# A second home for six eighths of the gate matrix of odd experts, the layer loop written out, and the router on column groups

## The chip, the cores and the metric

The kernel runs on one core of one Trainium2 chip. The metric is the time of one execution on the device in microseconds, the median of several runs. The engines named below are TensorE (PE in the profile, with its weight loads as PEld), VectorE (DVE), ScalarE (ACT), GpSimd (POOL) and SyncE (SP), which here only issues DMAs. SBUF is the on-chip memory of 128 partitions, PSUM the accumulators of TensorE, with eight banks of 512 float32 per partition. All data is float32.

## The reference

Two layers of a bidirectional encoder over 256 tokens of width 1024. Each layer adds a mixing block (latent attention with 16 heads, and a gated long convolution of order 2) and then a mixture of 16 experts, in which each expert picks its own 32 tokens:

```python
def expert_choice_ffn(h, router_w, wg, wu, wd):
    B, S, D = h.shape
    C = max(1, EC_CAPACITY_FACTOR * S // N_EXPERTS)
    aff = jax.nn.softmax((h @ router_w).astype(jnp.float32), axis=-1)
    gate, idx = lax.top_k(jnp.swapaxes(aff, 1, 2), C)
    flat_idx = idx.reshape(B, N_EXPERTS * C)
    xs = jnp.take_along_axis(h, flat_idx[..., None], axis=1).reshape(B, N_EXPERTS, C, D)
    a = jnp.einsum('becd,edf->becf', xs, wg)
    u = jnp.einsum('becd,edf->becf', xs, wu)
    o = jnp.einsum('becf,efd->becd', jax.nn.silu(a) * u, wd) * gate[..., None].astype(h.dtype)
    o = o.reshape(B, N_EXPERTS * C, D)
    return jax.vmap(lambda oi, ii: jnp.zeros((S, D), h.dtype).at[ii].add(oi))(o, flat_idx)

# per layer: x = x + merged @ w_out[l]
#            x = x + expert_choice_ffn(rms_norm(x, norm2_w[l]), router_w[l], wg[l], wu[l], wd[l])
```

Each expert has three matrices of 1024 x 1408, 1024 x 1408 and 1408 x 1024, that is 5632 KB each. With 2 x 16 experts the weights of the experts are most of what the kernel reads.

## The kernel before

**Memory.** `ring` (2 x 11264 columns per partition) holds units of the mixing block's weights first, and during the experts the gate matrix `wg` in its first half and the up matrix `wu` in its second. `region` (`R`, 12288 columns) holds q, k, v and the convolution's spectra first, and the down matrix `wd` during the experts (11264 columns). `attnT` (`aT`) holds the attention's output and later the normed x, transposed, which is the router's operand. `work` (`W`) is scratch of the mixing block; its last readers and writers before the experts are ScalarE's squares for the second norm (L885).

**Order.** Each engine has its own program, written out by hand with semaphores, and runs it in order. All five programs have a loop over the layers (`Fori(0, DEPTH)`) on registers. Inside, PE and VectorE loop over four groups of four experts, ScalarE over 16 experts, and SyncE over experts 1 to 15. Thresholds of waits that depend on the layer are computed in registers.

**Around the experts.** PE computes `merged @ w_out` (L644), transposes x (L629), and multiplies it with the router's weights: eight matmuls of 16 x 256 that accumulate in one bank (L654). VectorE copies the result (L1206), PE transposes it back (L660), VectorE takes the maximum (L1208, L1211), ScalarE the exponentials (L908), and VectorE picks the 32 best tokens of each expert (L1223 to L1234). Per group PE gathers the tokens of four experts with a matmul (L681). Per expert PE computes the gate product and the up product (both L695), each as eight steps of four matmuls on four column groups (a fp32 matmul counts as two instructions in the trace, so a product has 64), then two transposes of the selection (L703), three of the hidden rows (L709), the down product (L719) and the product that adds the rows to x (L734, L1273).

**SyncE's queue.** All weights are asked for by SyncE, in this order: gate(0) in two halves (L269) when w_out's first unit is used, up(0) (L272) when its second is used, then for e = 1 to 15 the first half of gate(e) after half of gate product e-1 (`gate_half`), its second half after the whole product (`gate_done`), up(e) after up product e-1 (`up_done`), and down(e) (L278) after down product e-1 (`o_psum`) in three pieces. down(0) is asked for earlier, before the last unit of w_out. At the end of a layer SyncE asks for the next layer's small tables, and for w_lat (L257) once `gate_done` has counted expert 15.

**Layer boundary.** After the last addition to x ScalarE squares x (L769), takes the root (L772), VectorE inverts it (L980) and scales x (L983), and PE transposes (L358).

## Time and profile before

| | us |
|---|---|
| median of 3 runs | 2113.52 |
| lowest and highest | 2112.22, 2116.02 |
| the profiled execution | 2112.32 |
| its span, first to last instruction | 2110.5 |
| PE busy in it | 1606.2 (76%) |
| DVE busy | 508.7 (24%) |
| ACT busy | 287.6 (14%) |
| moved by DMA | 644.83 MB, 306 GB/s over the span |

The page's map of the span in 40 slices shows two equal halves, one per layer. In each, PE is busy nine tenths and more while the DMA moves little, and then for some 600 us the DMA moves about 430 GB/s while PE is busy five or six tenths. The granted clock of PE is near full in the first kind of stage and eight or nine tenths in the second. Busy time of an engine says how long it had an instruction in it, not whether anyone waited for it; the chain that ended last says that. A wait named "issue" is time in which an engine waited for nothing that the profile shows.

### The profile page before, as it was taken

The page shows a single profiled execution, that of the slowest core. Times are in us where ns is not written, and L with a number is a line of the kernel's source. Part 1 is how long each engine was busy: PE and PEld are TensorE (multiplying, and loading weights), DVE is VectorE, ACT ScalarE, POOL GpSimd, SP SyncE. Part 2 cuts the span into 40 slices and gives each one's busy share as a digit, 9 for nine tenths or more (in the row PEclk, how much of TensorE's full clock was granted, in tenths as well). Part 3 has the DMA queues.
Part 4 walks back from the last instruction along what each step waited for, and adds up shares of the span by engine and source line. Part 5 has one row for each costly group of instructions (what it writes and reads, how often), then busy time and mean ns, then how long its engine had stood idle before and what let it go on. Part 6 is the DMA issues. An engine that isn't in the chain of part 4 may idle for free.

```text
span 2110.5 us, 23405 instructions
## 1 busy us (share of the span) xinstructions
PE 1606.2 (76%) x9552; PEld 909.9 (43%) x9552; DVE 508.7 (24%) x1057; ACT 287.6 (14%) x594; POOL 45.7 (2%) x24
## 2 busy tenths in 40 slices
PE   7999999876466566666689999997865665665665
PEld 4687688432232132232256866884322222321322
DVE  2654541111111111111126545402111111111111
ACT  2233200200000000000022332002000000000000
POOL 0300000000000000000002000000000000000000
PEclk9999999988788888878899999999887887888888
DMA  7522024679999999999945220246899999999997
GB/s 282 195 85 100 1 80 190 245 319 430 435 423 430 430 427 430 432 429 426 426 149 199 80 100 1 80 189 258 341 434 426 426 430 434 423 430 430 427 430 319
DMA packets 36352, 644.83 MB, mean 306 GB/s; under 512 B 3984, under 2 KB 4880, under 8 KB 6160
## 3 DMA queue, kind: packets, MB, share of 16 engines
q1 hardware_dynamic: 35472, 638.84, 72.2%
q10 hardware_dynamic: 768, 4.29, 0.7%
q8 instruction: 96, 1.57, 0.3%
q14 instruction: 16, 0.13, 0.0%
HBM read 642.07 MB, written 1.05 MB: 305 GB/s over the span
## 4 chain that ended last, share of the span: by engine, by line
PE 49%; DMA 42%; issue 4%; DVE 3%; DVEq 1%; SPq 1%; ACT 1%; ACTq 0%
DMA region<-w_down_dram 27%; DMA ring<-w_up_dram 15%; PE ps L695 7%; PE ps L394 7%; PE ps L619 5%; PE ps L461 5%; PE ps L719 3%; PE ps L644 3%; PE ps L552 2%; PE ps L681 2%; PE ps L587 2%; PE ps L577 2%; PE ps L422 2%; PE ps L484 1%; PE ps L439 1%
## 5 line engine op out<-in xcount | busy, mean ns | idle before, releaser
L695 PE MATMUL ps<-ring,uT 128*32 128x384 f32 (+1 forms) x4096 | 437.7, 567 | 296.8 <-DMA ring<-w_gate_dram 147.6
L695 PEld LDWEIGHTS ps<-ring,uT 128*32 128x32 f32 x4096 | 182.9, 130 | 550.6 <-issue 205.6
L719 PE MATMUL ps<-region,uT 128*32 128x512 f32 x1408 | 175.8, 596 | 34.9 <-DVE uT L1266 22.2
L1262 DVE TENSOR_TENSOR uT<-uT,ps 128x256 f32<-128x256 f32 x32 | 13.5, 421 | 699.4 <-PE ps L695 699.4
L394 PE MATMUL ps<-xnT,ring 128*128 128x256 f32 x768 | 178.3, 380 | 4.5 <-DVE uT L942 2.9
L394 PEld LDWEIGHTS ps<-xnT,ring 128*128 128x128 f32 x768 | 140.6, 190 | 24.1 <-DVE uT L942 4.5
L734 PE MATMUL ps<-uT 128*128 128x512 f32 x256 | 124.3, 618 | 28.8 <-ACT uT L926 28.8
L920 ACT ACT_TABLE_LOAD x32 | 41.1, 1283 | 631.3 <-PE ps L695 631.3
L461 PE MATMUL ps<-xnT,ring 128*128 128x256 f32 x512 | 115.0, 380 | 0.0
L719 PEld LDWEIGHTS ps<-region,uT 128*32 128x32 f32 x1408 | 44.5, 109 | 143.9 <-issue 105.3
L1273 DVE TENSOR_TENSOR x<-x,ps 128x512 f32<-128x512 f32 x128 | 87.9, 687 | 64.4 <-PE ps L734 64.4
L681 PE MATMUL ps<-uT,xnT 128*128 128x128 f32 x256 | 50.5, 381 | 68.2 <-issue 65.6
L461 PEld LDWEIGHTS ps<-xnT,ring 128*128 128x128 f32 x512 | 96.5, 190 | 13.7 <-issue 0.8
L734 PEld LDWEIGHTS ps<-uT 128*128 128x128 f32 x256 | 40.7, 188 | 114.9 <-issue 73.0
L681 PEld LDWEIGHTS ps<-uT,xnT 128*128 128x128 f32 x256 | 48.7, 294 | 73.7 <-issue 73.7
L1268 DVE COPY uT<-ps 128x512 f32<-128x512 f32 x32 | 22.1, 691 | 194.5 <-PE ps L719 194.5
L619 PE MATMUL ps<-uT,ring 128*128 128x256 f32 x256 | 57.9, 379 | 0.0
L619 PE MATMUL ps<-attnT,ring 128*128 128x256 f32 x256 | 57.9, 379 | 0.0
L644 PE MATMUL ps<-ring,uT 128*128 128x512 f32 x128 | 55.6, 592 | 0.0
L924 ACT ACTIVATE uT<-ps 128x256 f32<-128x256 f32 x32 | 12.3, 384 | 311.6 <-PE ps L703 311.6
L619 PEld LDWEIGHTS ps<-uT,ring 128*128 128x128 f32 x256 | 48.6, 190 | 6.6
L619 PEld LDWEIGHTS ps<-attnT,ring 128*128 128x128 f32 x256 | 48.6, 190 | 6.6
(195 smaller groups left out, 1368.1 us busy)
## 6 DMA issues: line engine op xcount, KB each, us to landing
ring<-w_gate_dram SPq DMA_DIRECT2D x64, 2816.0 KB, 28.4
ring<-w_up_dram SPq DMA_DIRECT2D x32, 5632.0 KB, 32.8
region<-w_down_dram SPq DMA_DIRECT2D x64, 2048.0 KB, 30.6
ring<-units_dram SPq DMA_DIRECT2D x34, 2048.0 KB, 8.0
region<-w_down_dram SPq DMA_DIRECT2D x32, 1536.0 KB, 37.2
ring<-w_lat_dram SPq DMA_DIRECT2D x4, 1344.0 KB, 20.6
ring<-w_q_b_dram SPq DMA_DIRECT2D x2, 2304.0 KB, 29.1
region<-filt_dram ACTq DMA_DIRECT2D x4, 512.0 KB, 11.9
```

Of the source, the lines that this page charges most:

```text
L394: m = mm(bank(b % 2, S), unit8(n)[:, i, j * P:(j + 1) * P], xnT[:, i], start=i == 0, stop=i == DB - 1)
L422: m = mm(bank((3 + g) % 7), latT[:, i, t * P:(t + 1) * P], m2[:, i, c * 512:(c + 1) * 512], start=i == 0, stop=i == QB - 1)
L461: m = mm(dst, unit8(7 + 4 * (i // 4) + g)[:, k, i % 4 * P:(i % 4 + 1) * P], xnT[:, k], start=k == 0, stop=k == DB - 1)
L552: m = mm(bank(5 + f), cst[:, C_F + t * NF + f * P:C_F + t * NF + (f + 1) * P], hflt[:, t], start=t == 0, stop=t == SB - 1)
L577: m = mm(bank(2 + f), cst[:, C_F + t * NF + f * P:C_F + t * NF + (f + 1) * P], z_t[:, c, t], start=t == 0, stop=t == SB - 1)
L619: m = mm(dst, unit8(n)[:, k, j * P:(j + 1) * P], (aT if g == 2 else uT)[:, k], start=k == 0, stop=k == DB - 1)
L644: m = mm(bank(4 + 2 * c + t), mT[:, k, t * P:(t + 1) * P], unit8(n)[:, k], start=k == 0, stop=k == DB - 1)
L681: m = mm(bank(i // 4, P, (i % 4) * P), xn2[:, t, i * P:(i + 1) * P], pick[:, t], start=t == 0, stop=t == SB - 1)
L695: m = mm(bank(b, QW[j], rows=CAP, row0=CAP * j), xs[:, i, q * CAP:(q + 1) * CAP], w[:, i, j * FT:j * FT + QW[j]], start=i == 0, stop=i == ...
L719: m = mm(bank(c, rows=CAP, row0=CAP * j), hT[:, b * P + CAP * j:b * P + CAP * (j + 1)], wd[:, CT * b + j, c * 512:(c + 1) * 512], start=b ...
L734: mm(bank(6 + k % 2), gselT[:, t * P:(t + 1) * P], o_sb[:, c * 512:(c + 1) * 512], start=True, stop=True).then_inc(s["y2_psum"], 1)
L1273: tt(xc, xc, bank(6 + k % 2), ALU.add).then_inc(s["x_dve"], 1)
```

## The change

The gate matrix of an expert is cut at six eighths: "a" are the weight rows i = 0 to 5 (8448 columns per partition), "b" the last two (2816 columns). Even experts keep a in the ring. Odd experts have it in a second home that starts behind the down matrix in `region` and runs through a spare area, `attnT` and `work`, which are laid out as one tensor with `region` for that. b and the up matrix keep their one place. SyncE asks for a(0), b(0) and up(0) as before, for a(1) once the router's matmul and the second norm are done (`lgT_psum`, `norm2_rms`), and then per expert for b, up, down and the a of the next expert. PE waits for a and b apart; `gate_a` takes the place of `gate_half`. To make room, the scratch for dynamic DMA descriptors is given as 2048 bytes.

The router's eight matmuls go to four column groups (weights padded from 16 to 32 columns), two on each; VectorE copies 128 rows, and a matmul with a constant matrix (C_SUM) adds the four groups and transposes in one. The loop over layers is a Python loop on every engine, and SyncE's loop over experts too.

```diff
@@ build
-        R = sb("region", 12 * 1024)
+        region = sb("region", 12 * 1024 + SPARE + DB * S + 3072)
+        R = region[:, 0:12 * 1024]
+        aT_t = region[:, 12 * 1024 + SPARE:12 * 1024 + SPARE + DB * S]
+        W = region[:, 12 * 1024 + SPARE + DB * S:12 * 1024 + SPARE + DB * S + 3072]
...
-        wg = ring[:, 0:SLOT].rearrange("p (i f) -> p i f", i=DB)
-        wu = ring[:, SLOT:2 * SLOT].rearrange("p (i f) -> p i f", i=DB)
+        wg_a = (ring[:, 0:A_COLS], region[:, NF_TILES * D:NF_TILES * D + A_COLS])
+        wg_b = ring[:, A_COLS:SLOT]
...
@@ block.sync
-            with sp.Fori(0, DEPTH) as L:
+            for L in range(DEPTH):
...
-                def load_gate(e, half):
-                    cols = slice(SLOT // 2 * half, SLOT // 2 * (half + 1))
-                    sp.dma_start(ring[:, cols], w_gate[L * E + e, :, cols]).then_inc(s["wg_in"], 16)
+                def load_gate_a(e):
+                    sp.dma_start(wg_a[e % 2], w_gate[L * E + e, :, 0:A_COLS]).then_inc(wga_in[e % 2], 16)
+
+                def load_gate_b(e):
+                    sp.dma_start(wg_b, w_gate[L * E + e, :, A_COLS:SLOT]).then_inc(s["wgb_in"], 16)
...
-                load_gate(0, 0)
-                load_gate(0, 1)
+                load_gate_a(0)
+                load_gate_b(0)
                 unit_is_used(16)
                 load_up(0)
-                with sp.Fori(1, E) as e:
-                    sp.wait_ge(s["gate_half"], L * E + e)
-                    load_gate(e, 0)
+                sp.wait_ge(s["lgT_psum"], L + 1)
+                sp.wait_ge(s["norm2_rms"], L + 1)
+                load_gate_a(1)
+                for e in range(1, E):
                     sp.wait_ge(s["gate_done"], L * E + e + FREE)
-                    load_gate(e, 1)
+                    load_gate_b(e)
                     sp.wait_ge(s["up_done"], L * E + e + FREE)
                     load_up(e)
                     sp.wait_ge(s["o_psum"], L * E + e + FREE)
                     load_down(e)
+                    if e < E - 1:
+                        sp.wait_ge(s["gate_a"], L * E + e)
+                        load_gate_a(e + 1)
@@ block.tensor
-                    m = mm(bank(4, S, rows=E), fvec[:, W_RT + i * E:W_RT + (i + 1) * E], aT[:, i],
-                           start=i == 0, stop=i == DB - 1)
+                    m = mm(bank(4, S, rows=EP, row0=EP * (i % 4)), fvec[:, W_RT + i * EP:W_RT + (i + 1) * EP], aT[:, i],
+                           start=i < 4, stop=i >= 4)
...
-                    m = tp(bank(5, E, t * E), lgT[:, t * P:(t + 1) * P], ident[0:E, 0:E])
+                    m = mm(bank(5, E, t * E), lgT[:, t * P:(t + 1) * P], cst[:, C_SUM:C_SUM + E], start=True, stop=True)
...
+                        pe.wait_ge(wga_in[q % 2], 8 * L * E + 32 * g + 16 * (q // 2) + 16)
+                        pe.wait_ge(s["sil_act"], n + FREE)
+                        for i in range(IA):
+                            m = product(2, wg[q % 2], i)
+                        m.then_inc(s["gate_a"], 1)
+                        pe.wait_ge(s["wgb_in"], 16 * (n + 1))
+                        for i in range(IA, DB):
+                            m = product(2, wg[q % 2], i)
+                        m.then_inc(s["gate_done"], 1)
@@ block.vector
-                copy(lgT, bank(4, S, rows=E)).then_inc(s["lgT_dve"], 1)
+                copy(lgT, bank(4, S)).then_inc(s["lgT_dve"], 1)
@@ kernel
-    nc = bacc.Bacc("TRN2", target_bir_lowering=False, num_devices=1)
+    nc = bacc.Bacc("TRN2", target_bir_lowering=False, num_devices=1, dynamic_dma_scratch_size=2048)
```

SyncE's program from gate(0) on, before. "ring<-w_gate_dram 128x5632" is half a gate matrix, and an ISA row is a wait of its own; the rows from the branch on are the loop over experts.

```order
L269 DMA ring<-w_gate_dram 128x5632 [waits wout_psum]
L269 ISA
L269 DMA ring<-w_gate_dram 128x5632
L247 REGISTER_ALU
L272 DMA ring<-w_up_dram 128x11264 [waits wout_psum]
L296 UNCONDITIONAL_BRANCH
L296 ISA
L269 ISA [waits gate_half]
L269 DMA ring<-w_gate_dram 128x5632
L299 REGISTER_ALU
L269 ISA [waits gate_done]
L269 DMA ring<-w_gate_dram 128x5632
```

The same place after. "128x8448" is a, "128x2816" is b, and "region<-w_gate_dram" is the second home.

```order
L278 DMA ring<-w_gate_dram 128x8448 [waits wout_psum]
L281 DMA ring<-w_gate_dram 128x2816
L284 DMA ring<-w_up_dram 128x11264 [waits wout_psum]
L278 DMA region<-w_gate_dram 128x8448 [waits norm2_rms,lgT_psum]
L281 DMA ring<-w_gate_dram 128x2816 [waits gate_done]
L284 DMA ring<-w_up_dram 128x11264 [waits up_done]
L290 DMA region<-w_down_dram 128x4096 [waits o_psum]
L290 DMA region<-w_down_dram 128x4096
L290 DMA region<-w_down_dram 128x3072
L278 DMA ring<-w_gate_dram 128x8448 [waits gate_a]
L281 DMA ring<-w_gate_dram 128x2816 [waits gate_done]
```

a(1) stands behind up(0) with waits for the router and the norm and no wait for a product, and a(2) behind down(1).

VectorE at the layer boundary, before: the last additions to x, the ends of the group loop and of the layer loop. The next instruction of the following layer is L980, 449 rows further up.

```order
L1273 TENSOR_TENSOR x<-x,ps 128x512
L1238 REGISTER_ALU
L1238 COMPARE_AND_BRANCH
L977 REGISTER_ALU
L977 COMPARE_AND_BRANCH
```

And after:

```order
L1298 TENSOR_TENSOR x<-x,ps 128x512
L1263 REGISTER_ALU
L1263 COMPARE_AND_BRANCH
L1005 RECIPROCAL small<-small 128x2
L1008 TENSOR_SCALAR region<-x,small 128x1024 x2
```

The reciprocal that starts a layer (L980 before, L1005 after) now follows the group loop directly.

## Rows read from the trace of the kernel before

**Rows 1.** The page: chain that ended last, shares by engine and line.

```profile
PE 49%; DMA 42%; issue 4%; DVE 3%; DVEq 1%; SPq 1%; ACT 1%; ACTq 0%
DMA region<-w_down_dram 27%; DMA ring<-w_up_dram 15%; PE ps L695 7%; PE ps L394 7%; PE ps L619 5%; PE ps L461 5%; PE ps L719 3%; PE ps L644 3%; PE ps L552 2%; PE ps L681 2%; PE ps L587 2%; PE ps L577 2%; PE ps L422 2%; PE ps L484 1%; PE ps L439 1%
```

**Rows 2.** Windows: us, busy us of engines, PEclk, DMA share, GB/s.

```profile
440.00:640.00 200.00, 131.68 (x1027) 53.52 (x1025) 28.44 (x57) 14.62 (x28) 0.00 (x0) 0.84 1.00 429
...
1500.00:1700.00 200.00, 131.38 (x981) 52.36 (x974) 29.95 (x58) 14.64 (x26) 0.00 (x0) 0.84 1.00 429
```

**Rows 3.** Pieces of that chain: start us, us, what.

```profile
466.18 8.02 PE ps L695 x34
...
1010.52 37.23 DMA region<-w_down_dram
```

**Rows 4.** Timeline of SyncE's DMA issues: start us, us, line, transfer, count.

```profile
409.20 0.33 SPq L272 DMA_DIRECT2D ring<-w_up_dram  x1
435.84 2.91 SPq L269 DMA_DIRECT2D ring<-w_gate_dram  x2
443.44 0.33 SPq L272 DMA_DIRECT2D ring<-w_up_dram  x1
...
1028.22 0.85 SPq L257 DMA_DIRECT2D ring<-w_lat_dram  x2
...
1486.98 2.91 SPq L269 DMA_DIRECT2D ring<-w_gate_dram  x2
1494.59 0.33 SPq L272 DMA_DIRECT2D ring<-w_up_dram  x1
```

**Rows 5.** Windows between router and expert 0; columns of rows 2.

```profile
422.00:424.00 2.00, 0.00 (x0) 0.00 (x0) 1.77 (x5) 0.00 (x0) 0.00 (x0) 0.50 0.83 360
424.00:436.00 12.00, 9.53 (x76) 8.02 (x79) 2.63 (x8) 0.00 (x0) 0.00 (x0) 0.73 0.01 1
436.00:438.00 2.00, 2.00 (x28) 1.00 (x24) 0.00 (x0) 0.00 (x0) 0.00 (x0) 1.00 0.64 169
...
1476.00:1488.00 12.00, 10.17 (x86) 8.34 (x90) 2.38 (x6) 0.00 (x0) 0.00 (x0) 0.76 0.05 13
```

**Rows 6.** Timeline, layer 0's router: start, us, what, [idle before <-releaser].

```profile
410.78 3.61 PE L654 MATMUL ps<-attnT,fvec 128*16 128x256 f32 x16 [0.17 <-issue]
411.33 0.84 ACT L892 ACTIVATE attnT<-ps,fvec 128x256 f32<-128x256 f32 x2
412.55 1.28 ACT L908 ACT_TABLE_LOAD   x1
412.57 0.17 DVE L1204 RECIPROCAL small<-small 128x2 f32<-128x2 f32 x1 [1.11 <-ACT small L903]
...
414.99 0.27 PE L660 MATMUL ps<-consts,uT 16*128 16x16 f32 x2 [0.60 <-DVE uT L1206]
...
415.56 0.16 DVE L1211 TENSOR_TENSOR small<-small 128x2 f32<-128x2 f32 x1
...
432.86 10.52 PE L695 MATMUL ps<-ring,uT 128*32 128x384 f32 x128 [0.97 <-DVE uT L1248]
```

**Rows 7.** Timeline, program's start and layer boundary; columns of rows 6.

```profile
11.42 0.17 DVE L980 RECIPROCAL small<-small 128x2 f32<-128x2 f32 x1 [10.54 <-ACT small L772]
...
1057.59 0.30 ACT L772 ACTIVATE small<-small,consts 128x2 f32<-128x2 f32 x1
1060.73 0.17 DVE L980 RECIPROCAL small<-small 128x2 f32<-128x2 f32 x1 [5.52 <-issue]
...
1062.46 3.38 PE L358 MATMUL ps<-consts,region 128*128 128x128 f32 x16 [7.97 <-DVE region L983]
```

**Rows 8.** Waits up to 432 us: who <- releaser: us, times, longest.

```profile
PE ps L495 <- issue: 0.6, 1, 0.6
DVE uT L1241 <- issue: 0.3, 1, 0.3
```

**Rows 9.** The page: the weights' DMA queue: packets, MB, share.

```profile
q1 hardware_dynamic: 35472, 638.84, 72.2%
```

More of the change, by code:

```diff
@@ L107, in build @@
         uT_t = sb("uT", 24 * S)
-        aT_t = sb("attnT", DB * S)
-        W = sb("work", 3072)
         cst = sb("consts", C_N)
@@ L311, in _ @@
         def _(pool):
-            with pool.Fori(0, DEPTH) as L:
+            for L in range(DEPTH):
                 pool.wait_ge(s["qkw_scaled"], L + 1)
@@ L350, in _ @@
                 pe.sem_inc(s[n], FREE)
-            with pe.Fori(0, DEPTH) as L:
+            for L in range(DEPTH):
                 pe.wait_ge(s["consts_in"], 16)
@@ L687, in _, with product @@
                         n = L * E + g * GROUP + q
-                        for w, b, arrived, read, done in ((wg, 2, "wg_in", "sil_act", "gate_done"),
-                                                          (wu, 3, "wu_in", "hid_dve", "up_done")):
-                            pe.wait_ge(s[arrived], (32 if w is wg else 16) * (n + 1))
-                            pe.wait_ge(s[read], n + FREE)
-                            for i in range(DB):
-                                for j in range(CT):
-                                    m = mm(bank(b, QW[j], rows=CAP, row0=CAP * j), xs[:, i, q * CAP:(q + 1) * CAP],
-                                           w[:, i, j * FT:j * FT + QW[j]], start=i == 0, stop=i == DB - 1)
-                                if w is wg and i == DB // 2 - 1:
-                                    m.then_inc(s["gate_half"], 1)
-                            m.then_inc(s[done], 1)
+                        def product(b, w, i):
+                            for j in range(CT):
+                                m = mm(bank(b, QW[j], rows=CAP, row0=CAP * j), xs[:, i, q * CAP:(q + 1) * CAP],
+                                       w[i][:, j * FT:j * FT + QW[j]], start=i == 0, stop=i == DB - 1)
+                            return m
+                        pe.wait_ge(wga_in[q % 2], 8 * L * E + 32 * g + 16 * (q // 2) + 16)
[7 more added lines that the diff above has]
+                        m.then_inc(s["gate_done"], 1)
+                        pe.wait_ge(s["wu_in"], 16 * (n + 1))
+                        pe.wait_ge(s["hid_dve"], n + FREE)
+                        for i in range(DB):
+                            m = product(3, wu, i)
+                        m.then_inc(s["up_done"], 1)
                         pe.wait_ge(s["gsel_dve"], n + 1)
@@ L756, in _ @@
                 act.sem_inc(s[n], FREE)
-            with act.Fori(0, DEPTH) as L:
+            for L in range(DEPTH):
                 load_sqrt_table()
@@ L976, in _ @@
             dve.sem_inc(s["x_dve"], X_FREE)
-            with dve.Fori(0, DEPTH) as L:
+            for L in range(DEPTH):
                 dve.wait_ge(s["norm1_rms"], L + 1)
```

23 lines of the change are left out of this document (17 added, 6 removed).

## The prediction

> **What bounds the kernel now.** I read the chain that ended last first: 49% of it is PE and 42% is DMA, and the DMA part is the expert weights, w_down and w_up [rows 1]. So there are two kinds of stage. Next the windows by stage: from 440 us to the end of layer 0's experts, and again from 1500 us in layer 1, the 16 DMA engines are busy 1.00 of the time and move 429 GB/s, while PE is busy about two thirds [rows 2]. The reader is to see that nothing PE does there matters as long as the queue never runs dry: the experts are a stream of bytes. One expert is 3 x 5632 KB = 17.3 MB, which at 429 GB/s is 40.3 us; the last piece of w_down in layer 0 lands 37 us after PE began to wait for it, at 1010.52 + 37.23 = 1047.75 [rows 3]. The other stages, some 420 us a layer, are PE's, and the DMA engines have little to do in them.
>
> So I look for the moment from which the stream runs without a gap, and for what comes before it. In the list of SyncE's DMA issues, layer 0 asks for up(0) at 409.20, and then for nothing until 435.84, when PE is half through gate product 0 [rows 4]. The windows show the consequence: the stream ends at about 423.7 (share 0.83 in 422 to 424), is 0.01 from 424 to 436, and is back in 436 to 438; in layer 1 the share of 1476 to 1488 is 0.05 [rows 5]. That is 13 us of idle queue in each layer, directly ahead of a stage that is nothing but queue. Every us of it that is filled with weights comes off the end.
>
> **The second home for the gate.** Call the six eighths "a" (4224 KB, 10.1 us at 429 GB/s) and the last two "b" (1408 KB, 3.4 us). Before, gate(1) (13.45 us) starts with the request at 435.84. After, a(1) may be asked for once the router's matmul has read attnT and the second norm has left "work". These end at about 414.4 and 412.5 [rows 6], well before up(0) has streamed out at 423.7, so a(1) queues behind up(0) without a gap and is through at 423.7 + 10.1 = 433.8. b(1) still waits for gate product 0 to end, and up(1) for up product 0. In the trace up product 0 ends 10.58 us after gate product 0 begins: begun at 432.86 [rows 6], up(1) asked for at 443.44 [rows 4]. b(1), asked for half-way through these 10.58 us, needs 1.4 us until its first data (as between the request at 435.84 and the 169 GB/s of 436 to 438 [rows 5]) and 3.4 us of stream, and so it is through by the time at which up(1) is asked for, or a few tenths before or behind it. From the request for up(1) on, the after-kernel streams without a gap.
>
> So before, the unbroken stream starts with a request at 435.84 and has gate(1) in it; after, it starts with a request at 443.44 less what the router gives (below, 1.45), at 442.0, and gate(1) is out of it. Gain: 13.45 - (442.0 - 435.84) = 7.3 us. Only 5.85 of it is the second home; it can't be the whole 10.1 us of a(1), because up(1) has a single home and becomes the next late thing. Layer 1 has the same distances (requests at 1486.98 and 1494.59 [rows 4], so 7.61 us between them as in layer 0). Two layers: 14.6 us.
>
> From expert 2 on I cost the second home at nothing. A load of up or down waits for the same event as before, b for the same as before's second half, and a(e+1) for an event that is long past when SyncE reaches it; the stream has no gap before [rows 2] and each request comes no later against it. Six DMAs per expert before, six after. What is queued behind SyncE's new waits is only expert weights.
>
> **The router on column groups.** Before, eight matmuls of 256 columns take 3.61 us one after the other, 0.45 each [rows 6]. After, four of them run side by side. The price is that of the expert products, which already do this: 16 steps of four (128 x 384) in 10.52 us, 0.66 a step, which is no more than one product of 384 columns at the router's pace (0.68). So a step of four costs 0.45. The first step starts at 410.78 as before, the second waits for ScalarE's copies, which end at 411.33 + 0.84 = 412.17, and ends at about 412.7 instead of 414.4. VectorE's reciprocal holds the next copy until 412.74 [rows 6]. The copy of 128 x 256 instead of 16 x 256 has as many elements per partition, and I take it to last as long. The two transposes (0.27 us) become two matmuls with 128 x 128 weights and 16 columns: at least nothing more, at most twice as long; I take 0.1. The exponentials need lmax (415.72 before) and the table load, which ends at 412.55 + 1.28 = 413.83 [rows 6]: with lmax at about 414.2 the table is not yet the next late thing. Saved: 1.45 us from here to gate product 0, counted above already. The top-k and the gather behind it are untouched.
>
> **The layer loop written out.** At the layer boundary ScalarE has the root of the norm at 1057.89, but VectorE takes it at 1060.73, with 5.52 us idle before it put down to "issue"; at the start of the program the same reciprocal waits for nothing but ScalarE's root [rows 7]. VectorE branches back over the whole layer there. Written out, the branch is gone and the 2.8 us with it, once. PE's transposes wait for exactly this [rows 7], and w_lat, asked for at 1028.22 [rows 4] and next in the stream behind w_down, has landed by then (2688 KB, 6.4 us of stream behind 1047.75). The inner loops over groups stay.
>
> The loop's register arithmetic goes too, some 40 instructions on PE per layer. Outside the experts the trace shows hardly any idle time put down to "issue" (0.6 us on PE, 0.3 on VectorE, each once up to 432 us [rows 8]), so I count zero, and at most 1 us a layer. From the other side a longer program could stall where it did not: one stall like VectorE's is 2.8 us. Both layers are straight code between the inner loops, and layer 0 is that already without such a stall, so zero again.
>
> The Trainium skill bears on both sides of this in "Runtime: NRT & Kernel Launch", section on the mechanics of instruction fetch: a sequencer streams straight code in blocks of 256 instructions, mostly hidden, and a taken branch to a target outside its two blocks waits for a fetch. By it the 2.8 us come back whole and rival 1 below falls away; the boundary's row agrees as far as VectorE goes, and ScalarE, which branches there too, shows no such wait. I keep the rival, since no trace shows straight code of twice this length.
>
> The larger tables (64 KB of router weights a layer, 8 KB of constants) come long before they are used.
>
> **Sum.** 14.6 + 2.8 = 17.4 us. The profiled execution took 2112.32 us with a span of 2110.5, so 2094.9 and 2093.1. The median of the runs, 2113.52, is 1.2 above the profiled one: 2096.1.
>
> **Rivals.** (1) The branch's time comes back in another form at the boundary (fetching new code, or PE not ready): 14.6 alone, 2098.9. Against it speaks the program's start [rows 7]. (2) More comes off: the waits of rows 8 and a few small ones on ScalarE and VectorE, up to 2 or 3 us a layer: about 2091. For it speaks that all four engines shed register work; against it that these rows are small.
> (3) The clock. PE runs the gather at the low level and is back at the high one only shortly before gate product 0: the granted clock is 0.73 over 424 to 436 and 1.00 in 436 to 438 [rows 5]. If the shorter router burst leaves PE at the low clock for products 0, a product takes 8.02 us as it does in mid-stream [rows 3] and not 5.3, up(1) is asked for 5.5 us later, and of 7.3 a layer 1.8 is left: 2 x 1.8 + 2.8 = 6.4 us, 2107.1. The same time comes out if a(1) is not in fact early, since then only router and branch are left (5.7). Against it speaks that the gather, the work that precedes the rise, is not changed.
> (4) Slower: a gap in the stream at every expert. The program gives the descriptors' scratch less room (2048 bytes, set by hand) and changes the piece sizes. If that made the queue drain once per expert, each drain costs the 1.4 us from request to first data, and from 17.4 / 30 = 0.6 us per expert on the change loses. One drain costs 30 x 1.4 = 42 us, so 2113.5 + 24.6 = 2138. Against it: all weights go by a queue of kind hardware_dynamic [rows 9], and SyncE runs several loads ahead of the landing in the trace.
> "SBUF — State Buffer" of the Trainium skill, section on the size of SBUF, calls this scratch the ring of the software-generated descriptors; by that page the weights' queue does not touch it and rival 4 has no ground but the piece sizes; no run here has shown it, and its chance stands as it is.
>
> **How the numbers follow.** Forecast 0.70 with 2091 to 2101 of its own (1 us of error a layer in each of the two terms, and 2 us between runs); rival 1 0.08; rival 2 0.10; rival 3 0.07; rival 4 0.04; 0.01 for anything else. Rivals 1 and 2 lie inside or at the edge, so 2089 to 2102 leaves out rivals 3 and 4 and the tails, about 2 in 10. A difference of 0.2% (4.2 us) is about what a measurement tells from none. Faster by more: the forecast, rivals 1 to 3, 0.93 after their tails; within it 0.03; slower 0.04.
>
> **What will show it.** Right: requests for a(1) near 413 and up(1) near 442.0, DMA share near 1.00 until 433.8, some 4 us idle and then 1.00; 429 GB/s after that; last w_down of layer 0 at about 1040.4 instead of 1047.75; at the boundary the reciprocal within 0.1 us of the root. Wrong: a share below 1.00 in mid-stream (rival 4), the clock at 0.5 in gate product 0 (rival 3), an "issue" wait at the boundary (rival 1), or stages outside the experts that are shorter by more than 1 us (rival 2).

## The result, and the profile after

| us | before | after |
|---|---|---|
| median | 2113.89 | 2086.93 (4 runs, 2084.02 to 2088.7) |
| the profiled execution | 2112.32 | 2086.2 |
| its span | 2110.5 | 2084.4 |

The ratio is 0.9877, with an interval of 0.9864 to 0.9889: 27.0 us less where 17.4 were forecast. 2086.9 lies below the range. So 9.6 us more came off than the steps of the prediction add up to.

Three stretches of each trace show where. The first runs from a layer's first transposes to the request for up(1), the second from there to the start of the last expert's product that adds rows to x, the third from there to the transposes of the next layer.

| us, layer 0 / layer 1 | before | after |
|---|---|---|
| transposes to the request for up(1) | 430.30 / 432.13 | 427.45 / 427.55 |
| from there to the last expert's addition | 607.16 / 606.89 | 601.01 / 596.59 |
| layer boundary | 11.86 | 8.97 |

The first stretch became shorter by 2.9 and 4.6 us, where the router's term is 1.45 in each layer.

The page of the kernel after, the map of the span, the queues and the chain that ended last:

```profile
span 2084.4 us, 22376 instructions
...
PEclk9999999988878888887899999999988888788888
DMA  7522024599999999999955220246999999999997
...
q1 hardware_dynamic: 35472, 638.98, 73.2%
...
q8 instruction: 57, 0.93, 0.2%
...
PE 49%; DMA 46%; DVE 2%; ACT 1%; issue 1%; DVEq 1%; ACTq 0%; SPq 0%
```

Against [rows 1], "issue" fell from 4% to 1%. The queue q8, which brings code, moved 57 packets, and in the kernel before:

```profile
q8 instruction: 96, 1.57, 0.3%
```

SyncE's DMA issues after (start us, us, queue, line, transfer, count), layer 0 and then layer 1, to set against [rows 4]:

```profile
408.83 0.33 SPq L284 DMA_DIRECT2D ring<-w_up_dram  x1
412.63 0.33 SPq L278 DMA_DIRECT2D region<-w_gate_dram  x1
436.04 0.33 SPq L281 DMA_DIRECT2D ring<-w_gate_dram  x1
441.20 0.33 SPq L284 DMA_DIRECT2D ring<-w_up_dram  x1
...
1478.73 0.33 SPq L284 DMA_DIRECT2D ring<-w_up_dram  x1
```

a(1) is asked for at 412.63, b(1) at 436.04 and up(1) at 441.20; 413, half-way to up(1), and 442.0 were forecast. The windows after (columns of [rows 2]):

```profile
424.00:426.00 2.00, 1.62 (x7) 1.65 (x8) 0.10 (x1) 0.00 (x0) 0.00 (x0) 0.50 0.94 406
426.00:434.00 8.00, 7.03 (x72) 5.48 (x75) 1.89 (x4) 0.00 (x0) 0.00 (x0) 0.91 0.95 408
434.00:436.00 2.00, 2.00 (x31) 1.02 (x25) 0.00 (x0) 0.00 (x0) 0.00 (x0) 1.00 0.00 0
...
440.00:442.00 2.00, 1.57 (x17) 0.54 (x9) 0.61 (x2) 0.38 (x1) 0.00 (x0) 1.00 0.51 211
442.00:444.00 2.00, 1.30 (x11) 0.55 (x15) 0.52 (x1) 0.00 (x0) 0.00 (x0) 1.00 1.17 360
440.00:640.00 200.00, 135.59 (x1028) 50.94 (x1020) 31.17 (x62) 15.02 (x27) 0.00 (x0) 0.86 1.00 427
1500.00:1700.00 200.00, 124.01 (x929) 47.20 (x925) 27.24 (x54) 14.04 (x25) 0.00 (x0) 0.84 1.00 430
```

The hole of 12 us in [rows 5] is filled up to 434. What is left is 434 to 436 and a dip to 0.51 before up(1). The clock is 1.00 in gate product 0, so rival 3 is out, and the stream runs at 427 and 430 GB/s, so rival 4 is out as far as this trace goes. At the boundary (timeline, columns of [rows 6]):

```profile
1049.03 0.30 ACT L797 ACTIVATE small<-small,consts 128x2 f32<-128x2 f32 x1
1049.36 0.17 DVE L1005 RECIPROCAL small<-small 128x2 f32<-128x2 f32 x1 [2.54 <-ACT small L797]
...
1051.18 3.65 PE L374 MATMUL ps<-consts,region 128*128 128x128 f32 x16 [5.09 <-DVE region L1008]
```

The reciprocal waits for the root alone. In [rows 7] it stood 2.8 us behind it.

The request, the filled hole and the boundary are the forecast. The largest part of what is left is in a place that the prediction never went to. PE's gather opens each round of the group loop (L681 before, L697 after). In the kernel before, at the three group boundaries of layer 0:

```profile
572.87 0.55 PE L681 MATMUL ps<-uT,xnT 128*128 128x128 f32 x1 [5.57 <-issue]
578.61 6.23 PE L681 MATMUL ps<-uT,xnT 128*128 128x128 f32 x31 [5.19 <-issue]
...
735.79 0.55 PE L681 MATMUL ps<-uT,xnT 128*128 128x128 f32 x1 [6.11 <-issue]
741.12 5.24 PE L681 MATMUL ps<-uT,xnT 128*128 128x128 f32 x31 [4.77 <-issue]
...
898.07 0.55 PE L681 MATMUL ps<-uT,xnT 128*128 128x128 f32 x1 [5.82 <-issue]
903.55 5.91 PE L681 MATMUL ps<-uT,xnT 128*128 128x128 f32 x31 [4.93 <-issue]
```

PE stands for 11 us at each with nothing to wait for. Packets of the code queue q8 lie in these waits: at the first boundary the trace has them at 569.8 and 576.2, each 1.0 us long, and PE goes on at 572.87 and 578.61. The kernel after at the same places:

```profile
560.62 3.81 PE L697 MATMUL ps<-uT,xnT 128*128 128x128 f32 x32 [1.37 <-DVE uT L1266]
...
726.38 5.57 PE L697 MATMUL ps<-uT,xnT 128*128 128x128 f32 x27 [6.32 <-issue]
...
889.14 6.64 PE L697 MATMUL ps<-uT,xnT 128*128 128x128 f32 x32 [6.57 <-issue]
```

The waits of PE, summed (who <- releaser: us, times, longest), before and then after:

```profile
PE ps L681 <- issue: 65.6, 12, 6.1
```

```profile
PE ps L697 <- issue: 13.1, 3, 6.6
```

Twelve waits at six boundaries have become three at two (6.3, 6.6 and 0.2 us), and layer 1 has none. PE has slack at these places (the experts are a stream of bytes), so 65.6 us of PE can't be 65.6 us of the program. What they cost the stream had to be measured.

### The profile page after: what moved, and what is told of

It reads as the page before. It is cut to its first block, busy times and chain, and to the rows that moved or that the text cites. A ratio compares the mean times of both kernels' runs of the same rounds, so it can differ in the third digit from the quotient of the medians.

```text
span 2084.4 us, 22376 instructions
## 1 busy us (share of the span) xinstructions
PE 1585.8 (76%) x9556; PEld 893.2 (43%) x9556; DVE 508.3 (24%) x1057; ACT 287.4 (14%) x594; POOL 45.7 (2%) x24
## 4 chain that ended last, share of the span: by engine, by line
PE 49%; DMA 46%; DVE 2%; ACT 1%; issue 1%; DVEq 1%; ACTq 0%; SPq 0%
DMA ring<-w_up_dram 43%; PE ps L707 12%; PE ps L410 7%; PE ps L635 5%; PE ps L477 5%; PE ps L660 3%; PE ps L568 2%; PE ps L603 2%; PE ps L593 2%; DMA region<-w_down_dram 2%; PE ps L438 2%; PE ps L500 1%; PE ps L455 1%; PE ps L744 1%; PE ps L383 1%; PE ps L524 1%
## 5 line engine op out<-in xcount | busy, mean ns | idle before, releaser
L707 PE MATMUL ps<-ring,uT 128*32 128x384 f32 (+1 forms) x3328 | 361.7, 559 | 288.3 <-DMA ring<-w_up_dram 254.5
L707 PEld LDWEIGHTS ps<-ring,uT 128*32 128x32 f32 x3328 | 146.8, 129 | 489.3 <-DMA ring<-w_up_dram 274.2
L707 PE MATMUL ps<-region,uT 128*32 128x384 f32 (+1 forms) x768 | 83.9, 571 | 46.2 <-DMA region<-w_gate_dram 46.2
L744 PEld LDWEIGHTS ps<-region,uT 128*32 128x32 f32 x1408 | 44.1, 109 | 151.4 <-issue 103.6
L707 PEld LDWEIGHTS ps<-region,uT 128*32 128x32 f32 x768 | 34.2, 130 | 98.0 <-DMA region<-w_gate_dram 57.8
L635 PE MATMUL ps<-region,ring 128*128 128x256 f32 x256 | 57.9, 379 | 0.0
L697 PE MATMUL ps<-uT,xnT 128*128 128x128 f32 x256 | 38.9, 323 | 21.1 <-issue 13.1
L951 ACT ACTIVATE uT<-ps 128x512 f32<-128x512 f32 x32 | 19.1, 597 | 237.2 <-PE ps L744 237.2
```

The lines of the kernel that those rows point to most:

```text
L635: m = mm(dst, unit8(n)[:, k, j * P:(j + 1) * P], (aT if g == 2 else uT)[:, k], start=k == 0, stop=k == DB - 1)
L707: m = mm(bank(b, QW[j], rows=CAP, row0=CAP * j), xs[:, i, q * CAP:(q + 1) * CAP], w[i][:, j * FT:j * FT + QW[j]], start=i == 0, stop=i == ...
L744: m = mm(bank(c, rows=CAP, row0=CAP * j), hT[:, b * P + CAP * j:b * P + CAP * (j + 1)], wd[:, CT * b + j, c * 512:(c + 1) * 512], start=b ...
```

## The experiments

Theory after the traces: PE's group loop doesn't fit in PE's store of code in the kernel before. After every branch back code is fetched again, and that costs the weights' stream a little each time. The change moved the loop in the program and so made it fit, in the profiled execution in layer 1 and at one boundary of layer 0. Rivals: the second home gives more than I worked out; the router gives more; fewer instructions of the layer loop help everywhere. Each group of experiments has its own measurement of the kernel before beside it, and its median moved between 2111.58 and 2113.89; differences between kernels of two groups are uncertain by that much.

How the loop lies can be counted in the compiled programs. One round is 1600 instructions with one gate home and 1598 with two; before, it stands at 3526 to 5125 of PE's program, after at 3468 to 5065 and 8525 to 10122. The Trainium skill, in "Runtime: NRT & Kernel Launch", section "Instruction fetch mechanics", gives PE room for 2048 instructions, filled in blocks of 256. So many instructions touch seven or eight such blocks, by where they start. Where the blocks begin I could only fit: with an offset of 52 instructions, which puts a block's edge behind the first matmul of the gather, where PE's second wait stands in the rows of before, the loop of before touches eight and those of after seven, the one of layer 0 by a hair (6.99 blocks from its first block's edge, and 6.75 in layer 1). 2048 instructions are eight blocks, and yet a loop over eight did not stay in any run below; why is open.

**The layer loop written out, alone.** The kernel before with `for L in range(DEPTH)` on all engines:

```diff
-            with pe.Fori(0, DEPTH) as L:
+            for L in range(DEPTH):
```

> The kernel before with nothing changed but the loops: the layer loop written out on all five engines and SyncE's loop over experts too. One gate home, old router. Theory A (what the forecast missed lies in the loops): about 4 us at the layer boundary (it was 3.96 in the trace of after, not 2.8), 1 us a layer outside the experts, and PE's stalls at the group boundaries (11 to 12 us of issue in each before, in two of six after) gone with some 1.3 us of stream each: together 9 to 12 us, so 2102 to 2105. Theory B (the missed part lies in the second home): only 2.8 to 4 us, so 2110 to 2111, and the stalls at the group boundaries stay.

Measured: 2100.74 against 2112.36, ratio 0.9945 (0.9931 to 0.9958), that is 11.6 us less and not 2.8. The boundary is 8.97 as after, the stretch of the experts 602.17 / 602.44, so 4.7 us a layer less, the code queue 39 packets, and no gather waits for issue.

**The second home, alone.** All of the change's `block.sync` and its products, with loops and router as before.

> The second home alone: layer loop on registers as before on all engines, old router; the scratch is 2048 bytes here too, since the room is needed. Theory A: 2 x 5.85 = 11.7 us, so 2102, with PE's stalls at the group boundaries as before and 429 GB/s. Theory B (the early request of a keeps the stream fuller all through): 17 to 21 us, so 2093 to 2097.

Measured: 2102.76 against 2112.36, ratio 0.9963 (0.9949 to 0.9978). Stretch of the experts 601.60 / 601.69, so 5.4 us a layer less, where 5.85 was worked out; boundary 11.77, 96 packets. The medians differ by 9.6 us, where 2 x 5.4 is 10.8. The stalls are there as before.

**The second home with its early request taken away.** The kernel after, in which a(1) is asked for only when gate product 0 has ended:

```diff
-                sp.wait_ge(s["lgT_psum"], L + 1)
-                sp.wait_ge(s["norm2_rms"], L + 1)
+                sp.wait_ge(s["gate_done"], L * E + 1 + FREE)
                 load_gate_a(1)
```

> The kernel after, but a(1) is asked for only when gate product 0 is done, directly ahead of b(1); everything else stays, the second home too. If the gain is the filled idle time, the stream starts with a(1) and b(1) at about 436.0 and reaches up(1) at 436.0 + 1.4 + 13.45 = 450.9 instead of 442.6: 8.3 us a layer are lost, so 2086.9 + 16.6 = 2103.5. If the second home gains in mid-stream, less is lost, 2090 to 2098.

Measured: 2104.68 against 2112.36, ratio 0.996 (0.9944 to 0.9976), 7.7 us below the kernel before where the kernel after is 27.0 below in the first measurement and 23.0 in the repeat further down: 15 to 19 us more. The stretch of the experts rises to 604.69 / 604.66 from the 596.6 that it has without stalls: 8.1 us a layer. Here a(1), 10.1 us of stream, is wholly behind the gap, so the early request is what the second home gives, and the layout by itself nothing: an expert takes 40.2 us from landing to landing here as in the kernel with one home and no stall.

**The code of the kernel before, moved by 20 instructions.** Here lies the test of the theory. The layer loop stays on registers, and PE gets 20 idle instructions at its start:

```diff
             with pe.Fori(0, DEPTH) as L:
+                for _ in range(20):
+                    pe.sem_inc(s["pad_pe"], 1)
```

> The kernel before with 20 idle instructions (increments of an unused semaphore) on PE at the start of a layer, where PE waits for x anyway. All loops stay. They shift PE's loop over the four groups (1600 instructions) by 20 places against the blocks of 256 in which its code is fetched. Theory F: the loop covers eight blocks before and seven when shifted, and only then stays in PE's buffer; so the stalls of 11 us at the six group boundaries vanish, the instruction queue moves about 42 packets instead of 96, and the stream gains 1.57 us at each boundary: 9.4 us, 2103.0. Theory G (the register arithmetic or the outer loop itself costs it): nothing changes, 2112.4.

Measured: 2102.73 against 2113.16, ratio 0.9954 (0.9938 to 0.9969). Work was added and 10.4 us came off. Stretch of the experts 602.51 / 602.50, 42 packets, boundary 12.36. From 562 to 1054 us, the last three rounds of layer 0, its code queue moves no packet at all; in the kernel before it moves nine in each of these rounds. The gathers at the group boundaries of this kernel:

```profile
570.62 3.81 PE L682 MATMUL ps<-uT,xnT 128*128 128x128 f32 x32 [1.43 <-DVE uT L1242]
...
731.69 3.81 PE L682 MATMUL ps<-uT,xnT 128*128 128x128 f32 x32 [1.43 <-DVE uT L1242]
```

**The other way: the written-out loop moved onto eight blocks.** The first experiment's kernel with 40 and 65 idle instructions:

```diff
+                for _ in range((40, 65)[L]):
+                    pe.sem_inc(s["pad_pe"], 1)
```

> The kernel with only the loops written out (2100.7 us), with 40 idle instructions on PE at the start of layer 0 and 65 at that of layer 1, so that PE's group loop covers eight blocks again in both layers. Theory F: stalls at all six boundaries come back, about 93 packets, 9.4 us slower, 2110. Theory G: 2100.7, no stall.

Measured: 2112.52 against 2113.16, ratio 0.9999 (0.9989 to 1.0008): all that the first experiment gained is gone. The experts take 606.76 / 606.71, the code queue 94 packets, and the stalls are back, after the ninth matmul this time, since the edge lies elsewhere in the loop:

```profile
572.78 2.26 PE L682 MATMUL ps<-uT,xnT 128*128 128x128 f32 x9 [6.58 <-issue]
577.93 5.28 PE L682 MATMUL ps<-uT,xnT 128*128 128x128 f32 x23 [2.89 <-issue]
```

The 65 idle instructions also cost at the boundary, which is 13.10 here and was 8.97. So about 4.1 us of this kernel is the padding's, and the stalls' share is the 4.6 + 4.3 us of the two stretches of experts. Together that is 13.0, and the medians differ by 11.8.

**Is it PE's lateness, or the fetch?** At a stall PE is 11 us late, so requests that hang on its products could be late too. Three memsets ahead of the last expert's additions in each group make PE late in the kernel whose loop fits:

```diff
+                        if q == GROUP - 1:
+                            for _ in range(3):
+                                nc.vector.memset(W[:, :], 0.0)
+                                dve.drain()
```

> The kernel with only the loops written out, with three memsets of the dead scratch (3072 columns each, 2 to 3 us) on VectorE ahead of the additions of the last expert of each group: PE is held up at every group boundary for 6 to 10 us, but fetches nothing. It tells what in a stall costs the stream. If it is the late requests of PE (a gap in the queue), the time between the landings around a boundary grows from 80.4 by 1.6 us for two experts, as in the kernel before. If it is the fetched code on the same DMA rings, the landings stay at 40.2 us each and only the delay of the last group of each layer shows in the time: 2100.7 plus twice the delay, 2113 to 2121.

Measured: 2118.95 against 2113.16, ratio 1.0034 (1.0019 to 1.0048); the stretch of experts 612.93 / 612.91, 10.6 us longer than in the first experiment. All of that is the last group's delay, which nothing hides: from the request for up(1) to the last landing of w_down it takes 599.4 us in both layers, as against 599.3 in the first experiment and 604.3 / 604.0 in the kernel before. Between the groups PE is as late as in a stall (from its last additions to its next gate product it takes 20.4 to 22.7 us, in the kernel before 21.5 to 22.7, in the first experiment 10.3 to 10.6), and the stream doesn't notice. The first row shows PE's wait at the third group boundary of layer 0, and the others the additions to x of experts 11, 12 and 13, which follow the landing of their last w_down:

```profile
900.15 3.78 PE L734 MATMUL ps<-uT 128*128 128x512 f32 x4 [8.72 <-DVE x L1277]
```

```profile
889.45 1.98 PE L734 MATMUL ps<-uT 128*128 128x512 f32 x4 [0.89 <-ACT uT L926]
...
930.81 3.88 PE L734 MATMUL ps<-uT 128*128 128x512 f32 x8 [0.89 <-ACT uT L926]
...
969.80 3.88 PE L734 MATMUL ps<-uT 128*128 128x512 f32 x8 [0.90 <-ACT uT L926]
```

The same three in the kernel before, and then in the kernel with the layer loop written out:

```profile
888.37 3.88 PE L734 MATMUL ps<-uT 128*128 128x512 f32 x8 [0.89 <-ACT uT L926]
...
929.54 3.88 PE L734 MATMUL ps<-uT 128*128 128x512 f32 x8 [0.90 <-ACT uT L926]
...
970.35 3.88 PE L734 MATMUL ps<-uT 128*128 128x512 f32 x8 [0.94 <-ACT uT L926]
```

```profile
886.29 3.88 PE L734 MATMUL ps<-uT 128*128 128x512 f32 x8 [0.89 <-ACT uT L926]
...
926.41 3.88 PE L734 MATMUL ps<-uT 128*128 128x512 f32 x8 [0.90 <-ACT uT L926]
...
966.62 3.88 PE L734 MATMUL ps<-uT 128*128 128x512 f32 x8 [0.90 <-ACT uT L926]
```

Two experts take 969.80 - 889.45 = 80.35 us with PE held up and 80.33 with PE free, but 81.98 with the stall. So a late PE costs the stream nothing, and what comes with the stall costs 1.6 us a boundary; by the stretches of the experts it is 4.3 to 5.0 a layer. In the kernel before, 96 - 42 = 54 packets more are fetched than with the 20 idle instructions, nine for each of six boundaries. They are not all fetched at the boundary: in the second round of layer 1 four lie in the first 30 us (1620.9 to 1645.6) and five in the 130 us behind (1671.3 to 1774.1). So code is fetched all through the round, while PE waits only at its start. The landings are late only with the four: the expert across the boundary takes 41.6 us from landing to landing, the next three 40.3, 40.2 and 40.2. So it is not the bytes: nine packets of 16 KB are 0.3 us of stream. How the fetches at the boundary hold the weights up by 1.6 us is not shown; the page's share of the DMA engines stays at 1.00 through it.

**The router, alone.** The kernel before with the eight matmuls on four column groups, the constant matrix, and the scratch of 2048 bytes. A first version without the smaller scratch has no time: a tensor of 1360 bytes per partition found 1216 left. Its expectation had 2.9 us, or 4.4 if the gather came off shorter too. The version that ran:

```diff
-                    m = mm(bank(4, S, rows=E), fvec[:, W_RT + i * E:W_RT + (i + 1) * E], aT[:, i],
-                           start=i == 0, stop=i == DB - 1)
+                    m = mm(bank(4, S, rows=EP, row0=EP * (i % 4)), fvec[:, W_RT + i * EP:W_RT + (i + 1) * EP], aT[:, i],
+                           start=i < 4, stop=i >= 4)
```

> The router on column groups alone, everything else as before (loops too), but with the descriptors' scratch at 2048 bytes, for room. From the trace of after, router to exponentials took 1.1 us a layer less, not 1.45: 2 x 1.1 = 2.2 us, so 2110.2. If the smaller scratch costs anything in the stream, as rival 4 of the forecast has it, slower than 2112.4.

Measured: 2110.32 against 2113.16, ratio 0.999 (0.9979 to 1.0). The interval reaches 1.0, so the time alone doesn't show a gain; the trace does. From the router's first matmul to PE's transposes of the softmax it takes 5.40 instead of 6.48 us, 1.1 a layer. In the kernel after (timeline):

```profile
410.41 0.64 PE L670 MATMUL ps<-region,fvec 128*32 128x256 f32 x8 [0.17 <-issue]
...
411.94 0.64 PE L670 MATMUL ps<-region,fvec 128*32 128x256 f32 x8 [0.90 <-ACT region L917]
...
413.21 0.59 PE L676 MATMUL ps<-consts,uT 128*128 128x16 f32 x4 [0.63 <-DVE uT L1231]
```

The two selecting matmuls take 0.59 us where 0.27 stood in [rows 6]; I had taken 0.1 more and the row has 0.3. The other part of the miss lies ahead of them: VectorE's copy was to start 1.96 us after the router's first matmul (412.74 - 410.78) and starts 2.23 us after it (412.64 - 410.41). The experts' stretch, 607.24 / 607.05, is that of before: the smaller scratch costs the weights nothing, with a stream that is never more full than here.

**The kernel after once more, and with its loops well inside seven blocks.** First the same kernel again, then with idle instructions so that its loops don't end at a block's edge (called e10 in the texts below):

```diff
+                for _ in range((80, 64)[L]):
+                    pe.sem_inc(s["pad_pe"], 1)
```

> The kernel after once more, beside the three that follow, for a like comparison and a second trace. 2086.9. PE's group loop of layer 0 ends within a few instructions of an eighth block there: some or all of its three boundaries should show the stall in this trace too, those of layer 1 none.

> The kernel after with 80 and 64 idle instructions on PE at the start of layers 0 and 1, so that both group loops begin just behind the start of a block and cover seven. Theory F: the stalls of layer 0 are gone for good, 39 to 42 packets, and the stretch from up(1) to the last product of layer 0 takes 596.6 us as in layer 1 and not 601.0: up to 4.4 us faster than the kernel after, 2082.5. If the kernel after doesn't stall in most of its runs, 2084 to 2086.

Measured, against 2112.05: 2089.03, ratio 0.9894 (0.9877 to 0.9911), and 2089.39, ratio 0.9896 (0.9879 to 0.9913). The repeat has no stall (39 packets, experts 596.83 / 596.63); the trace of the result above had two, and its experts of layer 0 took 601.01. So at a hair from the edge the loop fits in some executions and not in others, and the expectation of stalls here was wrong. The repeat gains more in the experts and yet less in all, 23.0 us and not 27.0: its stages ahead of up(1) took 430.68 / 430.40, where the first trace had 427.45 / 427.55. The padded kernel has 40 packets and 596.52 / 596.55, and pays at the boundary, 12.86 instead of 8.97, which its expectation of 2082.5 did not have; it is level with the repeat.

**Rolled loops, all else of the change, and 20 idle instructions.**

> Second home and new router, but the layer loop on registers as before on all engines, with 20 idle instructions on PE so that the group loop covers seven blocks. It tells what writing the layer loop out is worth by itself: the boundary takes 11.8 us instead of 9.0, so 2.9 us slower than e10, 2085.4. If written-out code gains more than that (registers), 2088 or more.

Measured: 2094.5, ratio 0.9914 (0.9898 to 0.993). Experts 597.76 / 596.71, boundary 12.44, 42 packets. This is the change without its written-out loop but with a loop that fits. It lies 5.1 us above the padded kernel after, and 2.9 were expected. The boundary can't be the reason, since it is the shorter one here, 12.44 against 12.86. The traces show the experts' 1.2 + 0.2, and 1.1 + 2.4 in the stages ahead of up(1). By the mark set before the run (2088 or more) this speaks for register work that costs something. The mixing block, whose matmuls are the same in all kernels, scatters by more than that (below), so the question stays open by a few us.

The five kernels with a rolled layer loop also show where the edge lies. Counted in the traces' rows of PE, the group loop starts at row 3510 to 3513 in the three that stall (the kernel before, the second home alone, the router alone) and at 3529 and 3533 in the two that don't, both padded by 20.

**Two versions for the gap that is left.** up(1) has one home, and is now the late thing. In the next kernel the b rows of the gate product come first, b(e+1) is asked for after them, a(e+2) after the whole gate product, and up in two halves of which the first is asked for after half the up product; PE's padding is as in the padded kernel, and the text after it calls this one e11.

```diff
-                    sp.wait_ge(s["gate_done"], L * E + e + FREE)
+                    sp.wait_ge(s["gate_b"], L * E + e)
                     load_gate_b(e)
+                    sp.wait_ge(s["up_half"], L * E + e)
+                    load_up(e, 0)
                     sp.wait_ge(s["up_done"], L * E + e + FREE)
-                    load_up(e)
+                    load_up(e, 1)
```

> e10 with the idle time between a(1) and up(1) filled as far as the order allows: gate product takes its last two rows first, so that b(1) is asked for 1.3 us into it instead of 5.3, and up is asked for in two halves, the first once half of the up product is done (438.6 instead of 441.2 in layer 0). The stream of up(1) then starts at 440.0 instead of 442.6. Predicted 2 x 2.6 = 5.2 us faster than e10: 2077.3. If seven DMAs per expert instead of six cost the stream anything, less.

Measured: 2086.68 against 2112.05, ratio 0.9882 (0.9865 to 0.9899). From gate product 0 to the last expert's addition it takes 605.38 / 605.61 us, against 607.10 / 607.13 in the padded kernel: 1.6 a layer. 2.6 were expected, and of the median 2.7 us came off where 5.2 were. An expert takes 40.29 us instead of 40.22 with its seven DMAs, which eats 1 us of what the earlier request gives.

Then the same with PE's padding where I took it to be hidden, under the wait for x at the start of layer 0:

```diff
-                for _ in range((80, 64)[L]):
+                for _ in range((128, 0)[L]):
```

> This is the kernel of e11 (the changed kernel with the b rows used first, b(1) asked for after two of them, and up(1) in two halves) with the idle TensorE instructions at one place only: 128 of them at the start of layer 0, ahead of the first transposes, where TensorE waits about 13 us for x; none stand at the boundary of the layers. Both group loops then lie within seven blocks of 256 instructions (6.5 and 6.2 blocks long from their first block's edge by the count that fits the other kernels). Theory (the boundary's 12.86 us of e11 against 8.97 us of the kernel after is the price of the idle instructions alone, and idle instructions of layer 0 lie under the wait for x): boundary 8.97, product-0-to-last-y2 605.4 and 605.6 us as in e11, 39 or 40 packets on the queue of instructions, time 2086.7 - 3.9 = 2082.8 us (2080 to 2086), below both kernels. Rival 1 (128 idle instructions, at some 60 ns each 7.7 us, are not hidden at the start): up to 2086.7. Rival 2 (one of the loops reaches an eighth block after all): 57 packets, 2 or 3 stalls at group boundaries of a layer and some 4.7 us more, 2087.5.

Measured: 2092.37 against 2111.58, ratio 0.9899 (0.9883 to 0.9915), slower than the one before it. The boundary is 8.97 as the theory had it, but 128 idle instructions are not hidden, and 2082.8 was missed by 9.6 us. PE's first transposes in this kernel, and in the one before it, whose 80 are hidden:

```profile
20.94 3.65 PE L381 MATMUL ps<-consts,region 128*128 128x128 f32 x16 [20.94 <-issue]
```

```profile
13.62 3.25 PE L381 MATMUL ps<-consts,region 128*128 128x128 f32 x16 [13.62 <-DVE region L1019]
```

They start 7.3 us later, so rival 1 of that run had the right mechanism; its 2086.7 was too low. The traces' other differences are 3.9 less at the boundary and 2.3 more ahead of up(1) in layer 0. No kernel here beats the kernel after by more than a measurement tells: the best, 2086.68, is level with its 2086.93 and 2.4 below its repeat, with intervals that overlap.

## Why the prediction was wrong, point by point

**The bound.** Right. Two kinds of stage, a stream of weights and PE's; every gain found is time taken from one of the two, and not a us came from making PE's work in mid-stream shorter.

**The second home, 5.85 us a layer.** Right in mechanism, and nearly in size: 5.4 measured alone. The request for a(1), the filled hole and the gap that stays are as forecast. The kernel without the early request gives the counter-proof: 8.1 us a layer more in the experts, where 8.3 were expected, and 15 to 19 us in all.

**The router, 1.45 us a layer.** The mechanism was right and a term was mis-sized: the selecting matmuls cost 0.3 more and not 0.1, the copy ahead of them starts 0.27 later than worked out, and altogether 1.1 came off.

**The written-out loop at the boundary, 2.8 us.** Right: 11.86 to 8.97 us, and the rule that I set beside it from the Trainium skill, "Runtime: NRT & Kernel Launch", section "Instruction fetch mechanics" (a taken branch out of the blocks waits for a fetch), agrees with both.

**"The inner loops over groups stay", "a longer program could stall", "so zero again".** This is the step that failed. I read a branch over a whole layer as a fetch, with the row of VectorE before me, and did not ask the same of the one inner loop that is long: PE's, of 1600 instructions, taken three times a layer. I looked for "issue" waits only up to 432 us [rows 8], where the change works, and the page's own chain had 4% of "issue" in it [rows 1], some 80 us, of which 49 are these waits at five of the six boundaries. And I took the order's numbers to have no meaning beside its rows: that the loop moved within the blocks is visible before any run, and nothing in the diff says it. The effect is 4.7 us a layer when all three stalls of a layer go, 9.4 in all. That this equals the miss of 9.6 is luck: in the profiled execution two stalls stayed. Its span is 26.1 us shorter, 8.7 more than forecast. The experts give 16.45, and less the second home's 2 x 5.4 that leaves 5.7 for the stalls. Another 4.5 is what the stages ahead of up(1) gave beyond the 2.9 forecast for the router (3.6 of it ahead of the router, where the matmuls are the same), and the repeat did not have it. The second home's 0.9 and a start later by 0.6 go the other way.

**"The stream has no gap before, so nothing from expert 2 on."** True of gaps, as the share of 1.00 says, and not true of speed. [rows 2] has 429 GB/s, and the same windows of the kernels without stalls have 426 to 430. The loss can't be seen there: 1.6 us in 160 is 1%, spread over windows that hold a boundary and much more. An expert's period from landing to landing (40.2 us, and 41.2 to 41.7 across a boundary) shows it, and I hadn't listed those.

**The sum now.** Second home 5.4 x 2, router 1.1 x 2, boundary 2.9, a loop that fits 4.7 x 2: 25.3 us if it fits in every execution. Median to median it is 27.0 in the first measurement and 23.0 in the repeat (2112.05 to 2089.03). The stages ahead of up(1) scatter by more than these differ: 427.5 to 434.6 us over the kernels that ask for up(1) at the same place. The mixing block alone, up to the router's first matmul, takes 396.2 to 402.4 us, without a relation to the edits that I can see. One place is in the rows below.

**The rivals.** 1, 3 and 4 did not happen. Rival 2, more comes off, named the right sign, and for its reason the register work; the kernel with 20 instructions more and all its register work refutes that reason for the stalls. The sign set for it, stages outside the experts that are shorter by more than 1 us, did show in the result's trace and was gone in the repeat; whether register work costs a few us besides is left open by the kernel with rolled loops.

## What to carry to other kernels

A loop body that comes near the size of an engine's store of code has a placement, and an edit ahead of it can make it fit or not fit, as 20 instructions did here with a loop of 1600. Before costing an edit, list "issue" waits over the whole span, look whether they stand at a loop's first instructions, and look at the packets of the instruction queue. Where two kernels differ in a saturated stream, compare the period from landing to landing, since a share of 1.00 hides a per cent.

## What the runs showed of the hardware that I had not expected

Twenty idle instructions on PE made the kernel before 10.4 us faster, and 40 and 65 in the two layers made the written-out one 11.8 us slower, 4.1 of it at the boundary. A loop of 1600 instructions that doesn't fit stalls PE at its start for 6 to 12 us and takes nine packets of 16 KB on the code queue in each round, one after another as PE goes through it; the weights' stream, on another queue, loses 1.6 us at the stall.

Idle `sem_inc` instructions are not cheap on PE: 64 of them cost 12.86 - 8.97 = 3.9 us at the boundary, in a place where PE had 5.09 us of slack. They fill the slack first, so the 60 ns each that I had taken is the wrong quotient. By my estimate it is 0.14 to 0.15 us: 64 lie in a wait of 8.98 us, and at the start 80 are hidden by 13.62 us while 128 end at 20.94, so 48 more take at least 7.3 us. The profile puts the wait down to issue (the kernel with 80 and 64):

```profile
1052.15 3.36 PE L375 MATMUL ps<-consts,region 128*128 128x128 f32 x16 [8.98 <-issue]
```

The clock scatters with the same instructions ahead of it. The latent products of layer 1 in the kernel after's repeat, and the window in it (columns of [rows 2]):

```profile
1054.39 7.73 PE L383 MATMUL ps<-ring,xnT 128*128 128x416 f32 x16 [0.97 <-DVE xnT L1014]
...
1055.00:1059.00 4.00, 4.00 (x8) 2.04 (x7) 0.00 (x0) 0.00 (x0) 0.00 (x0) 0.59 0.99 256
```

And in the first trace of the same kernel:

```profile
1055.80 5.83 PE L383 MATMUL ps<-ring,xnT 128*128 128x416 f32 x16 [0.97 <-DVE xnT L1014]
...
1056.00:1060.00 4.00, 4.00 (x12) 2.16 (x12) 0.00 (x0) 0.00 (x0) 0.00 (x0) 1.00 1.02 262
```

PE had the same transposes and the same gap of 0.97 us before both; the first was granted 0.59 over these 4 us, most of them at the lower level, 1.2 GHz, and the other 1.00, which is 2.4 GHz. That is 1.9 us at one place. A handful of such places per layer would make up the scatter of the mixing block; I have followed this one alone.
